# High-half products first in every weight block, with splits, scales and rows moved around the norms

## What is computed

```python
h = h + 0.5 * swiglu(rms_norm(h, g1), wg, wu, wd)
m = rglru_mixer(hn, ...) if i % 2 == 0 else pool_mixer(hn, pool_w, pool_b, pool_scale)
# pool_mixer: y = einsum('bsgc,gcd->bsgd', u, w); return (y + b) * scale
h = h + gate * (p @ ple_w_proj)            # gate = sigmoid(rms_norm(h, g) @ ple_w_gate)
```

## Time and profile before

| | |
|---|---|
| median of 3 runs | 1842.12 us (1840.05 to 1842.70) |
| the profiled execution itself | 1839.83 us |
| its span, first to last instruction | 1838.0 us |
| mean granted TensorE clock | 0.994 |
| busy: PE / DVE / ACT / POOL | 1774.6 / 1186.9 / 962.0 / 72.9 us |
| matmuls | 12462 |
| read from memory | 309.5 MB, 169 GB/s over the span |

### The profile page before, as it was taken

One profiled execution on the slowest core, in us unless ns is written; L12 is line 12 of the kernel. 1 busy time (PEld: TensorE's weight loads), 2 busy tenths in 40 slices (PEclk: granted clock), 3 DMA queues, 4 the chain that ended last, 5 costly groups with the idle time before them and its releaser, 6 DMA issues.

```text
span 1838.0 us, 29799 instructions
## 1 busy us (share of the span) xinstructions
PE 1774.6 (97%) x12462; PEld 1659.3 (90%) x12462; DVE 1186.9 (65%) x1471; ACT 962.0 (52%) x1141; POOL 72.9 (4%) x101
## 2 busy tenths in 40 slices
PE   6999999999999999899997999999999999999998
PEld 6999988999979999799986999889998999989997
DVE  5655677655566555755567888765556898875555
ACT  5554556644367444543456765454345866554443
POOL 9000000000000000100001000000000000000001
PEclk9999999999999999999999999999999999999999
DMA  8656434665545655355544544455664444356552
GB/s 216 224 179 199 152 128 151 214 206 183 186 158 166 207 182 183 104 194 183 185 161 151 178 139 138 134 178 183 189 192 153 153 161 138 120 171 192 186 179 91
DMA packets 229688, 311.86 MB, mean 170 GB/s; under 512 B 6568, under 2 KB 203040, under 8 KB 229472
## 3 DMA queue, kind: packets, MB, share of 16 engines
q1 hardware_dynamic: 225600, 304.11, 50.9%
q0 software_dynamic: 3840, 6.44, 1.4%
q10 hardware_dynamic: 160, 0.07, 0.0%
HBM read 309.54 MB, written 1.05 MB: 169 GB/s over the span
## 4 chain that ended last, share of the span: by engine, by line
PE 80%; DVE 9%; ACT 8%; issue 2%; DMA 1%; ACTq 0%; DVEq 0%
PE psA L1610 39%; PE psD L1636 25%; PE psA L1624 9%; ACT hi L419 3%; DVE lo L825 3%; PE psD L1874 1%; PE psA L1687 1%; PE psA L1636 1%; ACT xTh L449 1%; DVE xTl L852 1%; PE psD L1811 1%; DMA raw<-in_ffn_w_up 1%; ACT scr L485 1%; PE psA L1898 0%; PE psD L1687 0%
## 5 line engine op out<-in xcount | busy, mean ns | idle before, releaser
L825 DVE TENSOR_TENSOR lo<-raw,hi 128x2048 fp32r<-128x2048 f32 x287 | 655.7, 2290 | 332.0 <-ACT hi L419 331.7
L419 ACT ACTIVATE hi<-raw 128x2048 fp32r<-128x2048 f32 x287 | 545.8, 1910 | 335.2 <-PE psA L1610 203.8
L1610 PE MATMUL psA<-xTh,hi 128*128 128x256 f32 x2464 | 702.9, 285 | 11.9 <-DVE lo L825 10.4
L1610 PE MATMUL psA<-xTl,hi 128*128 128x256 f32 x2464 | 699.0, 284 | 0.0
L1610 PE MATMUL psA<-xTh,lo 128*128 128x256 f32 x2464 | 698.9, 284 | 0.0
L1610 PEld LDWEIGHTS psA<-xTh,hi 128*128 128x128 f32 x2464 | 474.5, 193 | 16.7 <-DVE lo L825 8.9
L1610 PEld LDWEIGHTS psA<-xTl,hi 128*128 128x128 f32 x2464 | 474.4, 193 | 2.1
L1610 PEld LDWEIGHTS psA<-xTh,lo 128*128 128x128 f32 x2464 | 474.3, 192 | 0.0
L1636 PE MATMUL psD<-hi,prod_hi 128*128 128x512 f32 x544 | 176.3, 393 | 1.9 <-DVE lo L825 1.9
L1636 PE MATMUL psD<-lo,prod_hi 128*128 128x512 f32 x544 | 175.1, 391 | 0.0
L1636 PE MATMUL psD<-hi,prod_lo 128*128 128x512 f32 x544 | 175.0, 391 | 0.0
(11 more groups left out here) (283 smaller groups left out, 1674.8 us busy)
## 6 DMA issues: line engine op xcount, KB each, us to landing
raw<-in_w_in SPq DMA_DIRECT2D x48, 1024.0 KB, 5.1
raw<-in_ffn_w_gate SPq DMA_DIRECT2D x44, 1024.0 KB, 5.3
raw<-in_ffn_w_up SPq DMA_DIRECT2D x44, 1024.0 KB, 5.3
raw<-in_ffn_w_down SPq DMA_DIRECT2D x44, 1024.0 KB, 4.9
raw<-in_w_gate SPq DMA_DIRECT2D x22, 1024.0 KB, 5.4
raw<-in_w_up SPq DMA_DIRECT2D x22, 1024.0 KB, 5.3
raw<-in_w_down SPq DMA_DIRECT2D x22, 1024.0 KB, 4.9
raw<-in_lru_w_in SPq DMA_DIRECT2D x10, 1024.0 KB, 5.1
```

Source lines behind the costliest of these rows:

```text
L419: act.activation(hi[:, n % RING, :], raw[:, n % RAW, :], ACT.Copy).then_inc(hi_ready, 1)
L825: dve.tensor_tensor(lo[:, n % RING, :], raw[:, n % RAW, :], hi[:, n % RING, :].bitcast(F32), ALU.subtract).then_inc(lo_ready, 1)
L1610: last = pe.matmul(to[:, f * S:(f + 1) * S], w[:, k, fs], x[:, k, :], start=(k == 0 and e == 0 and not (fresh and f)), stop=(k == KT - 1 a ...
```

## The change

It does seven things. (1) `features`, `tokens` and `contract` wait for the high half of the block first, do the 32 (or 16) products with `hi`, then wait for the low half and do the 16 (or 8) with `lo`; `contract_last` does so for its first three banks where columns are turned. (2) In a norm that has no gate, ACT makes `hi` of the next block between the turned pieces, and the calls that did this in the embedding stage go. (3) DVE updates h(0, second half) ahead of the second piece. (4) Behind the embedding stage ACT calls a Sigmoid on one column at the stage's end, PE's turns stand one bank later (`late=True`), and ACT's gates lie between pieces. (5) In the pooling stage pool_scale goes into the raw weights of the block (one DVE instruction in the feed-forward before it), the bias is added to h by four DVE instructions in place of GpSimd's two, and the update becomes one instruction in place of two. (6) In the first mix, the row of factors, its evacuations and softplus come one block later (ROW = 2). (7) At the double norm, h is rescaled behind the diagonal.

```diff
+        POOL_AT = sum(BLOCKS[s[0]] for s in plan[:[s[0] for s in plan].index("pool")])
+        ROW = (2, 1)
...
@@ gpsimd, pooling
-                    pool.wait_ge(rows_biased, 1)
-                    pool.wait_ge(h_ready, 2 * T * (updates + 1))
-                    for t in range(T):
-                        pool.tensor_tensor(xn[:, t, :], h[:, t, :], view(POOL_B, D), ALU.add).then_inc(rows_biased, 1)
@@ scalar: split, norm_rows, ple, mix
+                if n == POOL_AT:
+                    act.wait_ge(pool_scaled, 1)
...
                 piece(*parts[0], nth=st["gain"])
+                if gate:
+                    gate(0, 1)
                 piece(*parts[1], nth=st["gain"])
                 if early:
                     early(0)
                 if gate:
-                    gate(0, 1)
                     gate(1, 1)
+                elif not early:
+                    split_through(n_next)
                 piece(*parts[2], nth=st["gain"])
-                if before_last:
-                    before_last()
...
+                    act.activation(col(SPARE), eps[:, 1:2], ACT.Sigmoid)
...
-                        if i == 1:
+                        if i == ROW[l]:
                             soft(0)
-                        if i == 2:
+                        if i == ROW[l] + 1:
                             complement(0)
@@ vector: norm_pieces_of, norm_stats
                 piece(*parts[0], nth=st["gain"])
+                update(0, 1).then_inc(h_ready, 1)
                 piece(*parts[1], nth=st["gain"])
-                update(0, 1).then_inc(h_ready, 1)
                 update(1, 1).then_inc(h_ready, 1)
...
-                    for t, c in BY_ROWS:
-                        dve.tensor_scalar(h[:, t, half_of[c]], xn[:, t, half_of[c]], col(RSTD1 + t), None, ALU.mult).then_inc(h_ready, 1)
...
                         diagonal_of(t).then_inc(turner_ready, 1)
+                if rescale:
+                    for t, c in BY_ROWS:
+                        dve.tensor_scalar(h[:, t, half_of[c]], xn[:, t, half_of[c]], col(RSTD1 + t), None, ALU.mult).then_inc(h_ready, 1)
@@ vector: pooling
+            def scale_pool():
+                dve.wait_ge(pool_loaded, 48)
+                dve.wait_ge(raw_landed[POOL_AT % RAW], 16 * (POOL_AT // RAW + 1))
+                v = raw[:, POOL_AT % RAW, :].rearrange("p (g k d) -> p g k d", g=4, k=2)
+                s_ = view(POOL_S, 4, FC).unsqueeze(2).broadcast_to([P, 4, 2, FC])
+                dve.tensor_tensor(v, v, s_, ALU.mult).then_inc(pool_scaled, 1)
...
+                    st["update"](1, 1).then_inc(h_ready, 1)
+                    biased(0, 0)
+                    root(1)
+                    windows_of(1).then_inc(turner_ready, 1)
+                    biased(1, 0)
                     split_through(n + 1)
+                    piece(*pool_pieces[0], nth=st["gain"])
+                    biased(0, 1)
+                    piece(*pool_pieces[1], nth=st["gain"])
+                    biased(1, 1)
...
-                        step(dve.tensor_tensor(y, psD[:, 2 * t + c, :], view(POOL_S, D)[:, half_of[c]], ALU.mult))
-                        settle()
-                        dve.wait_ge(rows_biased, t + 2)
-                        return dve.tensor_tensor(h[:, t, half_of[c]], xn[:, t, half_of[c]], y, ALU.add)
+                        if (t, c) == (0, 0):
+                            dve.wait_ge(row_biased, 4)
+                        return dve.tensor_tensor(h[:, t, half_of[c]], psD[:, 2 * t + c, :], xn[:, t, half_of[c]], ALU.add)
@@ vector: the feed-forward's last blocks; mix
+                        if b == 1 and nxt[0] == "pool":
+                            scale_pool()
...
-                        if i == 1:
+                        if i == ROW[l]:
                             take_row()
-                            take_forget(0)
-                        if 1 <= i < FORGET:
+                            for done in range(i):
+                                take_forget(done)
+                        if ROW[l] <= i < FORGET:
                             take_forget(i)
@@ tensor: features (tokens is alike)
+                def high(f, k0, k1):
+                    for k in range(k0, k1):
+                        for x in (xTh, xTl):
+                            pe.matmul(to[:, f * S:(f + 1) * S], w_hi[:, k, f * P:(f + 1) * P], x[:, k, :],
+                                      start=(f == 0 and k == 0 and x is xTh), stop=False)
+
+                def low(f, k0, k1):
+                    for k in range(k0, k1):
+                        last = pe.matmul(to[:, f * S:(f + 1) * S], w_lo[:, k, f * P:(f + 1) * P], xTh[:, k, :],
+                                         start=False, stop=(f == 1 and k == KT - 1))
+                    return last
...
+                    else:
+                        pe.wait_ge(hi_ready, n_at)
+                    high(0, k0, k1)
+                    if fresh and k0 == 0:
+                        st["turns"](3)
+                    high(1, k0, k1)
...
+                    else:
+                        pe.wait_ge(lo_ready, n_at)
+                    low(0, k0, k1)
+                    last = low(1, k0, k1)
                 last.then_inc(block_used, 1)
@@ tensor: contract, contract_last, pooling, mix
+                pe.wait_ge(hi_ready, n_at)
+                for t in range(T):
+                    share(n, x_hi, x_lo, to, t, (0, 1), first, False, (0, 1))
                 pe.wait_ge(lo_ready, n_at)
                 for t in range(T):
-                    last = share(n, x_hi, x_lo, to, t, (0, 1), first, final)
+                    last = share(n, x_hi, x_lo, to, t, (0, 1), False, final, (2,))
...
-                    st["turns"](0)
+                    if not late:
+                        st["turns"](0)
                     share(n, *x, to, 1, (1,), first, False).then_inc(block_used, 1)
-                    st["turns"](1)
+                    if late:
+                        st["turns"](0)
+                    if not late:
+                        st["turns"](1)
                     share(n + 1, *y, to, 0, (1,), False, True).then_inc(rows_done, 1)
+                    if late:
+                        st["turns"](1)
...
-                        if (t, c) == (0, 1):
-                            st["turns"](0)
-                    st["turns"](1)
-                    st["turns"](2)
+                        if (t, c) != (0, 0):
+                            st["turns"](t + 2 * c - 1)
...
-                        if i == 1:
+                        if i == ROW[l]:
                             row_of_scales()
```

More of the change, by code:

```diff
@@ L1600, in features @@
                         xT_pieces(1 if k0 == 6 else 2)
[L1601 to L1612 removed]
+                    if n == 0 and k0 == 0:
+                        pe.wait_ge(first_hi, 1)
+                    elif n == 0:
+                        pe.wait_ge(hi_ready, 1)
+                    else:
+                        pe.wait_ge(hi_ready, n_at)
```

91 lines of the change are left out of this document (41 added, 50 removed).

## The result

The changed kernel took **1813.47 us** (median of 4 runs, 1812.69 to 1814.15) beside 1842.41 of the kernel before on the same chip: a ratio of 0.9845, 95% interval 0.9828 to 0.9862, 28.9 us less. Forecast were 1816.7 us, 25.4 less, in a range of 1811 to 1829. The profiled spans are 1838.0 and 1811.7 us, so 26.3 of it can be looked up place by place. The same kernel measured again, in the runs of the experiments, gave 0.9864 (0.9849 to 0.9880).

What follows compares the result with a forecast made beforehand. PE bounds the kernel, busy 1774.6 of 1838.0 us, so gains lie in its waits at transitions and the slow clock behind them. Terms per transition sum to 25.4 us: 1842.1 becomes 1816.7 us, range 1811 to 1829.

Steps and rivals of the forecast that it cites:

- High half first: Everywhere PE waits for lo: hi is ready 2.25 us or more earlier, so every such wait ends; added waits cost nothing.
- Start: Start of the program: third wait 1.9, restart 0.15, slow clock 1.87, small wait 0.4, less 0.2: 4.1 us won.
- Ordinary norms: Norms behind the two mixes: lo wait, restart and third turn's wait mostly go, diagonal comes earlier too: 1.4 us each.
- RG-LRU with the norm behind it: RG-LRU's entry and two waits for lo end, 3.8 us; the norm behind it gains 1.7.
- First embedding stage: Entry gains 1.0 us; exit gains 2.1 by an earlier table load, with new waits of 0.8, 0.7 and 1.5.
- Pooling: Pooling stage: wait of 3.7 becomes two of 0.7, slow clock goes at least once: 6.0 us, bounds 3 and 7.
- Second embedding stage, double norm, first mix: Entry gains 1.0; double norm and first mix 0.5, bounds -1.5 and +2, with a 7 us wait at the pair.
- Second mix: Ahead of the second mix: the ACT and DVE chain behind its lo and query waits starts 2.4 us earlier, gaining 2.4.
- A: The waits move on, since pieces, diagonal and softplus follow ACT and DVE chains: only 12.0 us won, 1830.1 us; chance 0.20.
- B: Each added mid-block wait costs PE 0.11 us, some 290 of them 32 us: slower, 1848.6 us; chance 0.05.
- C: The order doesn't matter at all, each earlier arrival ending in the next wait: 1842 us; chance 0.03.

Runs made afterwards that it cites:

- without parts 2 and 3: Changed kernel with ACT's next hi between turned pieces and DVE's earlier update of h's second half undone: 1825.66 us, ratio 0.9921 to the kernel before.
- without part 6: Changed kernel with the first mix's row of factors, its evacuations and softplus back behind block 1 (ROW = 1): 1815.63 us, ratio 0.9859 to the kernel before.
- without the Sigmoid: Changed kernel without the one-column Sigmoid at the embedding stage's end, turns still one bank later: 1815.84 us, ratio 0.9864 to the kernel before.
- early query: Changed kernel with first-layer pair products one block later, second query block evacuated earlier in both layers, and block 7's low half made earlier in the first: 1804.42 us.
- without part 1: Changed kernel with the high-half-first order of products undone and `late` kept: 1826.31 us, ratio 0.9923 to the kernel before.
- part 5 alone: Kernel before with only the pooling-stage change (scaled weights, bias on DVE, one-instruction update, turns one bank up): 1836.32 us, ratio 0.9979.
- part 1 alone: Kernel before with only the high-half-first order of products: 1829.95 us, ratio 0.9948.
- without part 4: Changed kernel without the Sigmoid at the embedding stage's end, turns at their old banks, both late gates behind the second piece: 1821.10 us, ratio 0.9896.

## Why the prediction was right

**The whole.** 25.4 us forecast, 26.3 in the profile and 28.9 by the medians (28.6 and 25 by the two ratios). The mechanism, waits taken from a PE that binds everywhere, is shown by the waits gone and by the runs that bring them back. The sums of the parts came out nearly as forecast; in two places, the start and the first mix, they did so by luck, as said below.

**High half first.** The added wait costs nothing, shown with 490 more. Every wait for `lo` ended. That made `hi` at the start the next thing, as written.

**Start, 4.1 forecast and 4.1 found, for half the reason.** Without the clock the sum had 2.25, as the end of the wait of 1.9. That wait is still there, 1.9 us long, now for `hi`; but `hi` is there at 41.31 where `lo` came at 43.77, 2.46 earlier, and PE is there earlier too. Ahead of it the first turns of x wait 2.1 less, by parts 2 and 3, and the first `lo` no longer 1.4, which the forecast did not have; the diagonal and `hi` take back what goes beyond the 2.46, and without parts 2 and 3 the start is 3.9 all the same. I put down another 1.87 for the slow clock as won by the change; this execution has 1.63 of it (7.34 - 5.71 us for the contraction). It isn't the change's to win: with part 1, PE waits 1.9 us for `hi` there in eight executions, and the clock fell in three of them (without part 6, without the Sigmoid, early query: 2.0 to 2.2 us won, not 4); in the three executions with a shorter wait, 0.9 to 1.4, it didn't. Of the three without part 1 it fell in two, and the third, part 5 alone, was 1.6 better for nothing. The window of the kernel without part 6 in which it fell:

```profile
42.00:46.00 4.00, 4.00 (x12) 3.10 (x11) 4.00 (x2) 1.39 (x1) 4.00 (x9) 0.57 0.33 45
```

So part 1 is worth 2 to 2.5 us at the start; whether it also makes the fall rarer, 3 in 11 against 2 in 3 can't tell.

**Ordinary norms**, 1.4 forecast, 1.3 found, each. In the norm of the earlier trace rows, ACT's timeline shows one `hi` in the gap between the second and the third piece, as laid out:

```profile
1385.73 1.14 ACT L450 ACTIVATE xTh<-psA,gain_col 128x128 fp32r<-128x128 f32 x4 [0.68 <-PE psA L1733]
1386.74 1.93 ACT L420 ACTIVATE hi<-raw 128x2048 fp32r<-128x2048 f32 x1
1388.94 1.14 ACT L450 ACTIVATE xTh<-psA,gain_col 128x128 fp32r<-128x128 f32 x4 [0.27 <-PE psA L1733]
```

The terms that I wrote down (0.83, 0.15, 0.3, 0.1) add up to the 1.4 only without the 0.2 to 0.3 that were to stay; no wait above 0.2 us is left in these norms. What I didn't see is that part 1 alone, or parts 2 and 3 without it, are each enough for nearly all of it; the second of them buys 0.2.

**RG-LRU with the norm behind it**, 5.5 forecast, 5.7 found: DVE's `lo` still come 6.33 us apart, and no wait for them is left, so the cover of 3.84 held for the three blocks.

**First embedding stage**, 3.1 forecast, 3.6 found, with waits of 0.49 and 0.38 where I had 0.8 and 0.7, and one of 0.78 at the row of factors where I had 1.5. The runs add that this needs all of them: without part 1 the entry loses 3.0, without parts 2 and 3, or without part 4, the exit loses nearly all of its 2.4.

**Pooling**, 6.0 forecast, 6.7 and 5.7 found, as the clock stays or falls there once. Part 5 carries 4.6 of it, slow clock included. The 1.0 that I gave to part 1 there is nothing: the table has 6.7 without it. Parts 2 and 3 have up to 1.0. The wait of 3.7 became one of 0.3 at the turn, and 1.5 for turned pieces came in front of it, where I had two of 0.7.

**Second embedding stage, double norm, first mix**, 1.5 forecast, 1.3 and 2.1 found, by luck: two errors of the sum cancel. The waits of 5.5 and 1.7 went and one of 6.7 came, with the clock at half behind it, as written, and the pair does hang on a chain that starts in the norm. But I had this chain end 1.9 earlier, for a `hi` of ACT moved out of it, with 0.4 for a softplus that comes later on DVE. It ends 0.0 earlier, 51.78 us behind the norm's first product in both kernels. With the row one block later, DVE makes one more `lo` (2.2) ahead of softplus, which starts 26.6 us behind that product where it started 24.1 behind it in the kernel before. The line of the kernel before, beside the one of 990.71 above:

```profile
1011.91 1.06 ACT L678 ACTIVATE scr<-scr 128x1024 f32<-128x1024 f32 x1 [5.35 <-DVE scr L1338]
```

ACT was idle for 5 to 6 us there in both, so a `hi` less ahead of it buys nothing at that place; what it buys behind it, the later start of softplus takes back. What the stretch did win is its entry (1.1) and the exit of the embedding stage (2.5), which comes through in full because the chain to the pair starts behind it, and which had no term of its own in the sum. The slow clock behind the pair took 2.3 and 1.6 of that, where I had 1.5. And inside this stretch part 6, which I took for a gain, is worth nothing in the changed kernel.

**Second mix**, 2.4 forecast, 2.4 and 1.5 found, the second with a longer stretch of slow clock: the wait for the query is 3.2 us in both, as PE catches up with a chain that starts earlier.

**The rivals.** A is what happens to part 1 alone (9.6 us) and fails for the whole, since parts 2 to 5 move the chains too. B is shown false by the run with the added waits. C, no change at all, is out by the result, whose interval ends at 0.9862.

## What to carry over

Before you count a long wait behind a place as a cushion for what is lost ahead of it, measure the distance from the event that starts its chain: if PE itself starts the chain, the wait travels with it, and only a cut of the chain helps. Measure it in kernels in which the candidates for that event moved against each other: five kernels here have 33.6 us from the row of factors, and only the others show that the norm is the start. Reorderings that each cover one engine's lateness are worth little one by one and more than their sum together, so take them out of the finished kernel one at a time, not only put them in. A result that is ready but whose evacuation stands behind waiting work in an engine's queue is the first thing to look for: moving two instructions gave 6.7 us more here than moving the consumer alone.

## What the runs showed of the hardware

Whether the granted clock falls behind a wait is chance to a good part. The changed kernel was run again with the expectation that the stretches of half clock lie in the same two places if the program fixes them, and in others if it is chance; they lay in the same two and in a third. Both executions have the same long waits (6.7, 4.3, 3.0, 1.9); in the second the clock was at half in pooling too, in this window, where the first has 1.00:

```profile
738.00:742.00 4.00, 4.00 (x27) 4.00 (x27) 1.82 (x5) 1.15 (x4) 0.00 (x0) 0.73 0.18 57
```

Behind the wait of 6.7 us it fell in all six executions that have it, and behind the same wait of some 1.9 at the start it fell in the kernel without part 6 and not in the changed one. One fall more cost 1 to 2 us of the span. A wait that is met costs TensorE less than 0.01 us (two more in a block left it at 3.83 + 1.92). An activation table's load costs its 1.28 us, of which 1.1 came onto the path, and no more.
